# The modulation sums at the entry of the second block: four tiles as split fp32r halves, and the sums ahead of the sums of squares

## The reference

```python
mod_lat = (jax.nn.silu(c) @ w_mod[i] + b_mod[i])[:, None, :]
mod_ctx = (jax.nn.silu(c_ctx) @ w_mod[i] + b_mod[i])[None, None, :]
sh1, sc1, gt1, sh2, sc2, gt2 = jnp.split(mod_lat, N_MOD, axis=-1)
hc = modulate(rms_norm_2(x_ctx, g_norm1[i]), csh1, csc1)   # h * (1 + scale) + shift
...
h = modulate(rms_norm_2(x_lat, g_norm1[i]), sh1, sc1)
...  # input projection h @ w_in, attention, mixing, MLP
```

## Time and profile before

| | us |
|---|---|
| median of 3 runs | 2676.57 |
| lowest and highest run | 2674.82, 2680.97 |
| profiled execution, its own time | 2674.22 |
| its span, first to last instruction | 2672.2 |
| TensorE matmul busy | 2605.0 |
| VectorE busy | 1669.5 |
| ScalarE busy | 1003.7 |

### The profile page before, as it was taken

The page is one execution under the profiler, slowest core; times in us unless marked ns, Lnnn a source line. Parts: engine busy times, 40 slices in busy tenths (PEclk is TensorE's granted clock), DMA queues, the critical chain, the costliest instruction groups (busy, mean ns, idle before and its releaser), DMA issues. The chain is left out here.

```text
span 2672.2 us, 44664 instructions
## 1 busy us (share of the span) xinstructions
PE 2605.0 (97%) x18839; PEld 2312.3 (87%) x18839; DVE 1669.5 (62%) x2246; ACT 1003.7 (38%) x1231; POOL 98.9 (4%) x179
## 2 busy tenths in 40 slices
PE   8999989999999999989999999999999999999999
PEld 8999888999999999789999954465899899747999
DVE  6887556778778877656787722462555555354555
ACT  4336401544344354114443321552433333153333
POOL 2110000000101100000001000000000000000000
PEclk9999988999999999989999999999999999999999
DMA  8776300656777775004557752101455655211452
GB/s 284 259 255 196 111 1 17 213 166 220 257 257 242 263 232 159 16 1 149 167 197 268 251 194 75 49 1 48 158 177 176 205 176 182 80 63 48 145 175 91
DMA packets 279510, 415.64 MB, mean 156 GB/s; under 512 B 10105, under 2 KB 235721, under 8 KB 277698
## 3 DMA queue, kind: packets, MB, share of 16 engines
q1 hardware_dynamic: 260332, 348.16, 39.6%
q0 software_dynamic: 18128, 64.20, 6.9%
q10 hardware_dynamic: 902, 1.15, 0.2%
HBM read 399.82 MB, written 13.65 MB: 155 GB/s over the span
## 5 line engine op out<-in xcount | busy, mean ns | idle before, releaser
L626 PE MATMUL ps<-h_high,w_low 128*128 128x256 f32 x2016 | 571.6, 284 | 0.0
L624 PE MATMUL ps<-h_high,w_high 128*128 128x256 f32 x1952 | 558.0, 286 | 6.7 <-DVE h_low L1444 4.7
L626 PEld LDWEIGHTS ps<-h_high,w_low 128*128 128x128 f32 x2016 | 388.1, 193 | 0.0
L624 PEld LDWEIGHTS ps<-h_high,w_high 128*128 128x128 f32 x1952 | 375.9, 193 | 8.7 <-issue 4.9
L1459 DVE TENSOR_TENSOR w_low<-ring,w_high 128x2048 fp32r<-128x2048 f32 x131 | 299.7, 2288 | 131.1 <-ACT w_high L1180 130.8
L625 PE MATMUL ps<-h_low,w_high 128*128 128x256 f32 x1312 | 372.5, 284 | 0.0
L2912 DVE TENSOR_TENSOR w_low<-ring,w_high 128x2048 fp32r<-128x2048 f32 x96 | 219.9, 2291 | 239.2 <-ACT w_high L2684 239.0
L1180 ACT ACTIVATE w_high<-ring 128x2048 fp32r<-128x2048 f32 x131 | 250.4, 1914 | 261.8 <-DMA ring<-in_ffn_w_in 143.6
L2684 ACT ACTIVATE w_high<-ring 128x2048 fp32r<-128x2048 f32 x96 | 183.8, 1916 | 329.9 <-PE ps L2339 304.3
L625 PEld LDWEIGHTS ps<-h_low,w_high 128*128 128x128 f32 x1312 | 253.2, 193 | 0.0
L1480 DVE SCALAR_TENSOR_TENSOR mod_acc<-wmod,cond,mod_acc 128x512 f32<-128x512 f32 x336 | 230.6, 744 | 0.0
(11 more groups left out here) (440 smaller groups left out, 5337.6 us busy)
## 6 DMA issues: line engine op xcount, KB each, us to landing
ring<-in_w_mlp SPq DMA_DIRECT2D x96, 1024.0 KB, 5.4
ring<-in_ffn_w_in SPq DMA_DIRECT2D x88, 1024.0 KB, 8.8
wmod<-in_w_mod POOLq DMA_DIRECT2D x96, 512.0 KB, 6.5
ring<-in_ffn_w_out SPq DMA_DIRECT2D x44, 1024.0 KB, 5.1
ring<-in_w_mix_in SPq DMA_DIRECT2D x26, 1024.0 KB, 5.4
ring<-in_xattn_w_kv SPq DMA_DIRECT2D x16, 1024.0 KB, 5.6
mod_scratch<-mod_acc POOLq DMA_DIRECT2D x24, 512.0 KB, 5.4
ring<-mod_scratch SPq DMA_DIRECT2D x12, 1024.0 KB, 6.7
```

Source lines behind the costliest of these rows:

```text
L624: mm(dst, w_hi, x_hi, start=start, stop=False, **more)
L626: return mm(dst, w_lo, x_hi, start=False, stop=stop, **more)
```

## The change

A copy of `one_row` in fp32r, `one_row_r`, is added. Four of the six modulation tiles (5, 0, 1, 2) are summed by the new `mod_sums_split`: ScalarE copies the tile to `w_high` (fp32r), VectorE subtracts it and writes `w_low` in place, and TensorE sums the two halves with two fp32r matmuls for each piece of 512 columns. There are two `w_high` buffers, so the third copy waits for the sums of the first split tile and the fourth for those of the second. On ScalarE the four copies stand ahead of the latents' logarithm, on VectorE the four subtractions stand ahead of the final-gain multiplies.

TensorE's order becomes: tiles 3 and 4 (float32), the latents' sums of squares, split tile 5, the transposes, split tiles 0, 1 and 2, the context's sums of squares, `mod_turn`, the latents' sums of squares. The shifts and scalings of layer 0 now run over all of the context and then all of the latents.

```diff
+        def mod_sums_split(part, final):
+            n = MOD_SLOTS[2 + part]
+            s, _ = place(("mod", 0, n))
+            pe.wait_ge(*mod_low.at(0, part + 1))
+            for m in range(SLOT // PIECE):
+                row, piece = n * (SLOT // PIECE) + m, slice(m * PIECE, (m + 1) * PIECE)
+                which = one_row_r[:, MOD_ROWS - 1 - row:2 * MOD_ROWS - 1 - row]
+                mm(ps[7][0:MOD_ROWS, :], which, w_high[part % 2][:, piece], start=False, stop=False)
+                last = mm(ps[7][0:MOD_ROWS, :], which, w_low[:, n, piece], start=False,
+                          stop=(final and m == SLOT // PIECE - 1))
+            last.then_inc(w_used[s].sem, 1)
...
-        mod_sums(0, MOD_SLOTS[2], False, False)
+        mod_sums_split(0, False)
...
-        for n in MOD_SLOTS[3:5]:
-            mod_sums(0, n, False, False)
-        for s in (CTX, LAT):
-            for q in range(4):
-                sums(0, 0, s, q)
-        mod_sums(0, MOD_SLOTS[5], False, True)
+        for part in range(1, 4):
+            mod_sums_split(part, part == 3)
+        for q in range(4):
+            sums(0, 0, CTX, q)
         mod_turn(0)
+        for q in range(4):
+            sums(0, 0, LAT, q)
...
+        for part in range(4):
+            n = MOD_SLOTS[2 + part]
+            s, _ = place(("mod", 0, n))
+            act.wait_ge(w_loaded[s].sem, 16)
+            if part >= 2:
+                before, _ = place(("mod", 0, MOD_SLOTS[part]))
+                act.wait_ge(w_used[before].sem, 1)
+            go(w_high[part % 2], store["ring"][:, n, :], ACT.Copy).then_inc(*mod_high.up())
         act.wait_ge(*turned.at(0, 1))
         go(std[:, LAT, :], ps[1][:, 0:T], ACT.Ln, bias=eps[:, 0:1], scale=1.0 / D).then_inc(*placed_act.up())
...
-                for k in range(KD):
-                    for s in (CTX, LAT):
+                for s in (CTX, LAT):
+                    for k in range(KD):
                         shift(i, 0, s, k)
...
+        step(0, v.memset(one_row[:, MOD_ROWS - 1:MOD_ROWS], 1.0), one_row_ready)
+        v.tensor_copy(one_row_r[:, :], one_row[:, :]).then_inc(*one_row_ready.up())
+        for part in range(4):
+            n = MOD_SLOTS[2 + part]
+            dve.wait_ge(*mod_high.at(0, part + 1))
+            v.tensor_tensor(w_low[:, n, :], store["ring"][:, n, :], w_high[part % 2], ALU.subtract
+                            ).then_inc(*mod_low.up())
         dve.wait_ge(*placed_act.at(0, 6))
...
-                for k in range(KD):
-                    for s in (CTX, LAT):
+                for s in (CTX, LAT):
+                    for k in range(KD):
                         scale(0, 0, s, k)
```

More of the change, by code:

```diff
@@ L2066 @@
     "sm2_norm": 96, "sm2_act": 48, "pt2_done": 48, "pt2_ready": 48, "av2_done": 48, "av2_out": 12,
-    "placed_act": 6, "mla_sq": 12, "mla_std": 14, "mla_dve": 29, "key_gain_ready": 3, "one_row_ready": 2, "mod_turned":
+    "placed_act": 6, "mla_sq": 12, "mla_std": 14, "mla_dve": 29, "mod_high": 4, "mod_low": 4, "key_gain_ready": 3, "one_row_ready": 3, "mod_turned":
     1
@@ L2393, in mlp @@
             mlp_order(tiles, pe, tile, lambda step, j, q: None)
-        pe.wait_ge(*one_row_ready.at(0, 2))
+        pe.wait_ge(*one_row_ready.at(0, 3))
         for n in MOD_SLOTS[0:2]:
@@ L2940, in vector_program @@
         step(0, v.memset(one_row[:, :], 0.0), one_row_ready)
-        v.memset(one_row[:, MOD_ROWS - 1:MOD_ROWS], 1.0).then_inc(*one_row_ready.up())
+        step(0, v.memset(one_row[:, MOD_ROWS - 1:MOD_ROWS], 1.0), one_row_ready)
[5 more added lines that the diff above has]
+                            ).then_inc(*mod_low.up())
         dve.wait_ge(*placed_act.at(0, 6))
@@ L3155, in scaled_at @@
     def scaled_at(i, n, s, k):
-        return 2 * KD + KD * streams(i).index(s) + k + 1 if n else KD * s + k + 1 if i else 2 * k + s + 1
+        return 2 * KD + KD * streams(i).index(s) + k + 1 if n else KD * s + k + 1
     def h_at(i, s, k):
@@ L3180, in build_second @@
     one_row = sb("one_row", [P, 2 * MOD_ROWS - 1])
+    one_row_r = ctx.enter_context(nc.sbuf_tensor("one_row_r", [P, 2 * MOD_ROWS - 1], F32R))
+    mod_high, mod_low = sig("mod_high"), sig("mod_low")
     one_row_ready, mod_turned = sig("one_row_ready"), sig("mod_turned")
```

## The result

| | before | after |
|---|---|---|
| median, nine runs each | 2677.15 us | 2684.93 us |
| lowest and highest run | 2674.82, 2681.14 | 2678.83, 2690.32 |
| profiled execution, its span | 2674.22, 2672.2 | 2678.83, 2676.8 |
| TensorE busy | 2605.0 | 2597.5 |

The ratio is 1.0028 with a 95% interval of 1.0017 to 1.0039, that is 4.6 to 10.4 us slower. TensorE's busy time fell by 7.5 us, and the kernel became slower. The forecast was 2680.4 us with a range of 2675.5 to 2685.5: the median lies in the range, near its upper end.

The account below looks back on a forecast made before the run. TensorE, busy 97%, was taken as the bound, with the input projection's start deciding. Queue +2.3 us plus low clock +1.5 gave +3.8: 2678.0 us for the profiled execution, 2680.4 by the median; range 2675.5 to 2685.5.

Parts of the forecast that it names:

- The bound and the queue: Second block's entry: final gain and context copies wait behind four subtractions, ending 7.8 us later; projection starts 2.3 us later.
- The price of a split matmul: Split modulation tiles: 0.23 us per 512-column fp32r matmul, 1.84 us a tile, 6.8 us less TensorE work over four tiles.
- The copy of `one_row`: Tiny VectorE copy ahead of the first modulation sum: delays TensorE's start by 0.15 us (0.1 to 0.2).
- The slack of the side chain: VectorE context copies and ScalarE context squares, beside TensorE's sums: about 3.6 us before TensorE needs them.
- The low clock at the context sums: After 4.7 us of TensorE idle ahead of the context sums, a half-speed phase costing 1.5 us.
- The rule that the prediction took from the Trainium skill: Waits let the array slow, so every burst starts slow: each of the two idles in the entry costs.
- Then unchanged work: From the input projection's first matmul, expected at 1588 to 1591 us, to the end: no further change.
- The forecast at full clock: Entry of the second block without the added low clock: projection starts at 1588.2 instead of 1585.96 us, +2.3 us.
- A: Context sums: same order, no slow clock there; +2.3 us, 2678.9 us; chance 0.25.
- B: Both norm sums (L2296): clock stays low through them; +5.5 to +9 us, 2682 to 2685.6 us; chance 0.15.
- C: Entry: TensorE remains the bound, projection starts at 1579.3 us; 2669.9 us; chance 0.06.
- D: Split tiles: a split matmul costs as fp32, 0.44 us; +3.4 us on top, 2683.8 us; chance 0.03.

Follow-up runs that it names:

- The trace of 2684.95 us: The changed kernel unaltered, its fourth trace: execution 2684.95 us, span 2682.9, mean clock 0.981, second block's start to projection 43.13 us, projection to end 1092.7.
- the orders alone: Kernel before with the change's new TensorE order and shifts and scalings by stream, all six modulation tiles float32, no split: 2680.96 us, ratio 1.0011.
- side work first: Changed kernel with the logarithm and exponential ahead of copies 2 and 3, final-gain multiplies and parameter and context copies ahead of subtractions 2 and 3: 2679.46 us, 1.0015.
- two and three split tiles: Kernel before, old order, tiles 5 and 0 split: 2675.72 us, 0.9990; tile 2 also split, summed last, side work behind exponential and context copies: 2672.98, 0.9987.
- its first wait filled: Changed kernel with 18 float32 matmuls of constant ones ahead of the context sums only: 2679.09 us, ratio 1.0002 against the kernel before.
- filling the ladder: Kernel before with 3 matmuls of constants ahead of the turn and 10 behind it, in TensorE's idle before the projection: 2676.72 us, ratio 1.0000.
- with the ladder filled: Kernel with three tiles split, plus 3 matmuls of constants ahead of the turn and 10 behind it: 2672.80 us, ratio 0.9978 against the kernel before.

## Why the prediction was right, and where not

**The bound and the queue: right.** The input projection's start decides, and it moved by what stands behind the copies and subtractions. Each step, counted from the block's first instruction (before minus 1547.81, after minus 1548.83; the forecast's times minus 1547.81):

| step | forecast | after |
|---|---|---|
| first sum starts | 0.7 | 0.77 |
| split tile 0 ends | 13.2 | 13.3 |
| copy 3 starts | 17.2 | 17.14 |
| final gain starts | 21.4 | 21.3 |
| context squares start | 27.4 | 27.2 |
| context sums start | 28.0 | 27.9 |
| latent sums end | 37.1 (35.6 at full clock) | 37.1 |
| projection starts | 41.9 (40.4 at full clock) | 41.8 |

The price of a split matmul was forecast at 0.23 us and measured at 0.23. That is also near the 215.7 ns that the Trainium skill's page "TensorE: Matmul & The Clock Gate", section "Wait — 56ns, not 53.3ns?", gives for 512 columns; the trace has 0.23, and so the trace's figure stands. The copy of `one_row` delayed the first sum by 0.23 us, not 0.15: the small cast takes 0.20. (The slack of the side chain was read with 1571.5 where the row has 1571.60; it is 3.66 us.)

**The low clock at the context sums: its place right, its size too small.** In the four traces of the changed kernel these sums took 5.25, 6.09, 6.44 and 6.57 us instead of 3.65; the loss is 1.6 to 2.9 us where the forecast had 1.5. The entry came to +3.67, +4.5, +4.9 and +5.0 us. The rule that the prediction took from the Trainium skill, "TensorE: Matmul & The Clock Gate", section "HAM oscillation — how this bites in real kernels", that each wait is followed by slow work, is borne out at both long waits of the first trace (0.50 in 1577 to 1579 and in 1591 to 1593). The two shorter waits ahead of split tiles 2 and 3, 0.68 and 1.67 us, were followed by matmuls at the full pace of 0.23 us.

**"Then unchanged work": the step that failed.** The sum ended at the projection's start and put all that follows at nothing. In the first trace that held (1086.2 us in both). In the median it doesn't. By the profiled execution the forecast was +3.8 and the trace +4.6, of which 1.0 lies ahead of the block. By the medians it was +3.8 (2680.4 us) and the measurement +7.8, or +7.5 by the ratio. The trace of 2684.95 us shows what can lie between them: the rest was 6.5 us longer, with a granted clock of 0.54 to 0.56 in two stretches in which TensorE had no more idle than usual. The clock averaged over all executions tells the same: 0.9809 and 0.9805 for the changed kernel, 0.9835 for the one before. Over all timed kernels, executions of one kernel lie near a line of 1.75 us of span for 0.001 of mean clock (1.2 to 2.4 for single kernels). Taken to the same clock of 0.984 by that line, an estimate, the changed kernel is 2.6 to 2.7 us slower than before, the orders alone +0.7, side work first -0.4, two and three split tiles -3.2 and -5.1. The forecast at full clock had +2.3 for the changed kernel; with the slopes of single kernels the estimate is anywhere from +1 to +4, so this agrees but is no sharp test.

**Rivals.** A (no low clock at the context sums) fell with the first trace. B gave 2682 to 2685.6 us, and 2684.93 lies in that; but its mechanism didn't occur. The low clock ended within the context sums each time and the latent sums took 3.66 to 3.67 us. The time came from another place, so this was no hit for B. And the range holds the median in part by luck, since its upper end, 2685.5, was B's. C (TensorE stays the bound) and D (0.44 us a matmul) fell with the chain and with the 0.23. The measured loss is 0.28% (0.17 to 0.39); slower by over 0.2% had 0.25, a change within 0.2% had 0.68. The error was to price the added idle by the one low phase that the trace of before showed right behind its idle, and not to ask what the clock does in the stretches behind.

**What stays open.** Shown is that most of the extra low clock goes when either long wait is filled: that takes 7 to 8 us away, of which the entry's steps and the projection's start explain 1.5 to 2.9. That it goes because TensorE is no longer idle is the likely reason, but it is argued: no run put the same matmuls where there is no wait. Against a simple count of waits speaks that the orders alone, with one long wait ahead of the projection, have a mean clock of 0.9823, and the changed kernel with its first wait filled, with the same one left, 0.9840. The difference is about two and a half times its standard error (12 executions each, in different groups). Why the low clock comes up to 150 us later, and why filling the ladder does nothing for the kernel before, stays open too.

## What to carry to other kernels

Idle time on a helper engine is not free to use where work that others wait for stands behind it in program order: ask of each inserted instruction what it waits for, and who waits for what is queued behind it. Here the first two copies and subtractions cost nothing and all four together ended the context copies 7.6 us later, in a chain with 3.7 us of slack. Splitting three tiles, with the last subtraction behind the copies that others wait for, started the projection 4.9 us sooner than before; with the ladder filled that kernel is the only one here that is faster than before clear of noise. And a change that gives TensorE idle time must be timed over many executions, for one trace, and the quickest execution at that, can show half of the loss.

## What the runs showed of the hardware

Executions of one and the same program on one core differed by up to 13.6 us (2676.48 to 2690.04 us, 12 executions), and they went with the mean granted clock, 0.986 to 0.978. Low clock was granted also in the midst of work without idle (11 us at 0.54 with TensorE wholly busy), and in the same kernel not at the same places. A fill of 18 small float32 matmuls of constants, 4 us of useless work in a wait of 4.4 or 4.7 us, made the changed kernel 7 to 8 us quicker; 13 of them on the kernel before's ladder gave it nothing.
